# Adding every expert block's result to one line per token in DRAM, and the last LayerNorm's statistics on ACT

## What is computed

```python
def moe_ffn(h, ...):                 # t: 1024 tokens x 1024
    scores = sigmoid(t @ w_router)   # 64 experts
    _, idx = top_k(scores + router_bias, 8)
    gate_w = 2.5 * sel / sel.sum(-1)
    ...                              # pairs (token, expert), sorted by expert, in blocks of 128
    yb = (silu(g) * u) @ w_expert_down[e]          # g, u from xblk @ w_expert_gu[e], 256 each
    routed = segment_sum(yb * row_w, row_tok)      # 8 lines are added per token
    shared = (silu(sg) * su) @ w_shared_down
    return routed + shared
y = moe_ffn(modulate(layer_norm(x1), shift, scale), ...)
out = layer_norm(ALPHA * x1 + gate * y) * ln2_g + ln2_b
```

## Time and profile before

| | us |
|---|---|
| median of three runs | 1880.53 |
| the profiled execution | 1878.81 |
| its span | 1877.0 |
| TensorE busy | 1775.9 (95%) |
| VectorE busy | 1126.2 (60%) |
| ACT busy | 763.3 (41%) |
| GpSimd busy | 726.1 (39%) |
| GpSimd's DMA queue (q0) | 73.57 MB, 15.3% of 16 engines' span |
| SP's queue (q1) | 298.45 MB, 41.8% |

### The profile page before, as it was taken

The page is one execution under the profiler, slowest core; times in us unless marked ns, Lnnn a source line. Parts: engine busy times, 40 slices in busy tenths (PEclk is TensorE's granted clock), DMA queues, the critical chain, the costliest instruction groups (busy, mean ns, idle before and its releaser), DMA issues.

```text
span 1877.0 us, 33114 instructions
## 1 busy us (share of the span) xinstructions
PE 1775.9 (95%) x7478; PEld 1247.1 (66%) x7479; DVE 1126.2 (60%) x1653; ACT 763.3 (41%) x1043; POOL 726.1 (39%) x753
## 2 busy tenths in 40 slices
PE   6999999998889999899999999999999999999966
PEld 1546454446754465478887888888888878888823
DVE  4751766403868644657628898563965784555428
ACT  0210111222230021356638788563865774655400
POOL 2000000004822224635545565554654554555513
PEclk9999999999999999999999999999999999999978
DMA  9752000011343323668648899673987897678794
GB/s 381 268 207 91 1 0 0 0 36 40 113 164 147 144 112 88 195 237 331 241 157 323 313 361 370 236 262 99 359 271 236 278 356 214 189 223 253 221 321 190
DMA packets 113533, 376.76 MB, mean 201 GB/s; under 512 B 34858, under 2 KB 35018, under 8 KB 102739
## 3 DMA queue, kind: packets, MB, share of 16 engines
q1 hardware_dynamic: 65696, 298.45, 41.8%
q0 software_dynamic: 46640, 73.57, 15.3%
q10 hardware_dynamic: 1156, 4.21, 0.6%
HBM read 349.31 MB, written 130.40 MB: 256 GB/s over the span
## 4 chain that ended last, share of the span: by engine, by line
PE 78%; DMA 6%; DVE 5%; issue 3%; ACT 2%; POOL 2%; SPq 1%; DVEq 1%; ACTq 1%; POOLq 0%
PE psum L1286 9%; PE psum L1288 8%; PE psum L1287 8%; PE psum L1029 7%; PE psum L1134 5%; PE psum L1273 4%; PE psum L1307 4%; PE psum L1305 4%; PE psum L1306 4%; PE psum L1038 4%; DMA raw_weights<-in_w_gu 4%; PE psum L1347 3%; PE psum L987 3%; PE psum L1069 3%; PE psum L1188 2%
## 5 line engine op out<-in xcount | busy, mean ns | idle before, releaser
L1796 DVE TENSOR_TENSOR split_weights<-raw_weights,split_weights (+1 forms) x366 | 428.1, 1220 | 34.0 <-ACT split_weights L692 32.2
L692 ACT ACTIVATE split_weights<-raw_weights (+1 forms) x366 | 364.2, 1062 | 21.0 <-SPq L491 12.1
L1286 PE MATMUL psum<-split_weights,split_rows 128*128 (+1 forms) x832 | 334.9, 402 | 0.6 <-DVE split_rows L1785 0.6
L1288 PE MATMUL psum<-split_weights,split_rows 128*128 (+1 forms) x832 | 325.5, 391 | 0.0
L1287 PE MATMUL psum<-split_weights,split_rows 128*128 (+1 forms) x832 | 324.1, 390 | 0.0
L692 ACT ACTIVATE arena<-psum 128x1024 f32<-128x1024 f32 (+4 forms) x200 | 161.3, 811 | 397.6 <-PE psum L1029 107.1
L655 POOL DMA_INDIRECT pair_rows<-arena,idxs x104 | 200.2, 1925 | 35.1 <-issue 31.7
L692 ACT ACTIVATE split_rows<-psum 128x256 fp32r<-128x256 f32 (+1 forms) x209 | 148.4, 710 | 153.4 <-PE psum L1294 150.7
L1288 PEld LDWEIGHTS psum<-split_weights,split_rows 128*128 128x128 f32 x832 | 156.2, 188 | 34.6
L1286 PEld LDWEIGHTS psum<-split_weights,split_rows 128*128 128x128 f32 x832 | 156.9, 189 | 29.6 <-DVE split_rows L1785 0.8
L1287 PEld LDWEIGHTS psum<-split_weights,split_rows 128*128 128x128 f32 x832 | 156.8, 188 | 29.8
(11 more groups left out here) (261 smaller groups left out, 2453.7 us busy)
## 6 DMA issues: line engine op xcount, KB each, us to landing
raw_weights<-in_w_gu SPq DMA_DIRECT2D x62, 2048.0 KB, 11.0
raw_weights<-in_w_dn SPq DMA_DIRECT2D x62, 1024.0 KB, 9.3
arena<-in_w_ada SPq DMA_DIRECT2D x12, 2048.0 KB, 8.8
arena<-pair_rows SPq DMA_DIRECT2D x16, 1024.0 KB, 11.1
arena<-in_toks SPq DMA_DIRECT2D x18, 512.0 KB, 9.8
arena<-job_rows SPq DMA_DIRECT2D x16, 512.0 KB, 3.7
arena<-in_w_vog SPq DMA_DIRECT2D x1, 4160.0 KB, 12.7
arena<-in_w_qk SPq DMA_DIRECT2D x1, 4096.0 KB, 17.8
```

The costliest lines, as they stand in the source:

```text
L692: return act.activation(o, i, ACT.Copy)
L1286: mm(bank(3 + p), xk, part(par, 0, 512 * k), start=(k == 0), stop=False)
L1288: ins = mm(bank(3 + p), xl, part(par, 0, 512 * k), start=False, stop=(k == 7))
L1796: tt(cols(wsplit, (1 - par) * (2 * WE) + (WE + 1024 * c), 1024), cols(raw, (1 - par) * WE + 1024 * c, 1024), high, ALU.subtract).then_inc( ...
```

## The change

- **One line per token.** `y_dram` has 1,024 rows. SP stores the shared expert's tile into it (line 481), and every block adds its rows to it with an accumulating indirect DMA; nothing is stored by blocks. An add waits until the add of the block before has landed. One index column serves gather and add.
- **Order on GpSimd.** Per block: gather of block b+5 first, then the add of block b. Before the loop it waits for the shared lines' stores.
- **No scaling of the shared weights, no `add_shared`.** The lines of `x1_dram` are loaded as they are.
- **The end.** SP loads one line per token (8 transfers of 512 KB). TensorE has nothing to do. VectorE multiplies by the gate row and adds the residual in place; ACT makes the sum of a tile with one pass (`accum_out`), the negative mean, and the sum of squared differences with a second pass; GpSimd makes the reciprocal root; VectorE normalises as before. SP issues the output in ACT's place.

```diff
-                sp.dma_start(shared_dram[P * j:P * j + P, :], yB[:, j % 2, :]).then_inc(S(f"acc_out{j % 2}"), 16)
+                sp.dma_start(y_dram[P * j:P * j + P, :], yB[:, j % 2, :]).then_inc(S(f"acc_out{j % 2}"), 16)
...
             for j in range(NTX):
-                load_pairs(j)
+                sp.dma_start(yres[j], y_dram[P * j:P * j + P, :]).then_inc(S(f"y_in{j}"), 16)
+            for j in range(NTX):
+                sp.wait_ge(S("out_ready"), j + 1)
+                sp.dma_start(out[P * j:P * j + P, :], yres[j]).then_inc(S("out_done"), 16)
...
-            pool.tensor_scalar(g2S, g2S, 1.0 / ALPHA, None, ALU.mult).then_inc(S("prepared"), 1)
-            pool.tensor_tensor(wsd, wsd, g2S.unsqueeze(1).to_broadcast([P, 2, D]), ALU.mult).then_inc(S("prepared"), 1)
-            for j in range(3):
-                add_shared(j)
...
             for q in range(64):
-                if q in (24, 40, 62):
-                    add_shared(3 + (24, 40, 62).index(q))
...
-            def scatter(b, p, nth):
+            def add_rows(b, p, nth, before):
 
                 pool.wait_ge(S("m_y"), b + 2)
-                pool.tensor_copy(idxs[:, 2 * p:2 * p + 2].unsqueeze(2), idxS[:, :].rearrange("p (v n) -> p v n", v=2)[:, :, bass.ds(b, 1)]).then_inc(S("idx_copied"), 1)
+                pool.tensor_copy(idxs[:, p:p + 1], idxT[:, bass.ds(b, 1)]).then_inc(S("idx_copied"), 1)
                 pool.wait_ge(S("idx_copied"), nth)
+                pool.wait_ge(S(f"added{1 - p}"), before)
                 pool.sem_inc(S("passed"), 1)
-                pool.indirect_dma_start(out=y_dram[0:NSUM, :], out_offset=..., in_=yB[:, p], ...).then_inc(S(f"stored{p}"), 16)
-
-            def add_rows(p, before):
-
-                pool.wait_ge(S(f"stored{1 - p}"), before)
-                pool.indirect_dma_start(out=y_dram[0:NSUM, :], ..., compute_op=ALU.add).then_inc(S(f"added{p}"), 16)
+                pool.indirect_dma_start(out=y_dram[:, :], ..., compute_op=ALU.add).then_inc(S(f"added{p}"), 16)
...
+            for i in range(2):
+                pool.wait_ge(S(f"acc_out{i}"), 64)
             with pool.Fori(0, rest) as i:
                 for p in range(2):
 
-                    scatter(2 * i + p, p, 4 * i + (2 * p + 6))
                     pool.wait_ge(S("m_xb"), 2 * i + (p + 4))
-                    gather(bass.ds(2 * i + (p + 5), 1), 1 - p, 4 * i + (2 * p + 7))
-                    add_rows(p, 16 * i + (16 + 16 * p))
-            add_shared(6)
-            add_shared(7)
+                    gather(bass.ds(2 * i + (p + 5), 1), 1 - p, 4 * i + (2 * p + 6))
+                    add_rows(2 * i + p, p, 4 * i + (2 * p + 7), 16 * i + (16 + 16 * p))
...
             for j in range(NTX):
-                act.wait_ge(S("out_ready"), j + 1)
-                act.dma_start(out[P * j:P * j + P, :], yres[j]).then_inc(S("out_done"), 16)
+                act.wait_ge(S("y_ready"), j + 1)
+                act.activation(squares[j % 2], yres[j], ACT.Copy, accum_out=ysum[:, j:j + 1]).then_inc(S("y_step"), 1)
+                act.wait_ge(S("y_step"), 2 * j + 1)
+                act.activation(ymean[:, j:j + 1], ysum[:, j:j + 1], ACT.Copy, scale=-1.0 / D).then_inc(S("y_step"), 1)
+                act.wait_ge(S("y_step"), 2 * j + 2)
+                act.activation(squares[j % 2], yres[j], ACT.Square, bias=ymean[:, j:j + 1], accum_out=yvar[:, j:j + 1]).then_inc(S("y_mv"), 1)
...
-            def combine(j):
-                        ins = mm(o, ident, ybuf[HALF * (j % 4) + k][:, 512 * h:512 * h + 512], start=(k == 0), stop=(k == HALF - 1))
...
             for j in range(NTX):
                 y = yres[j]
-                dve.wait_ge(S("ysum_pe"), j + 1)
-                tt(y, psum[:, 0:1024] if j % 2 == 0 else psum[:, 1536:2560], g2B, ALU.mult).then_inc(S("ysum_read"), 1)
-                link(stt(y, x1_in[j], ALPHA, y, ALU.mult, ALU.add))
-                moments(y, mv[:, 2 * j:2 * j + 2], "y_mv", hst[:, 8:20] if j % 2 else stats)
+                dve.wait_ge(S(f"y_in{j}"), 16)
+                link(tt(y, y, g2B, ALU.mult))
+                stt(y, x1_in[j], ALPHA, y, ALU.mult, ALU.add).then_inc(S("y_ready"), 1)
                 if j >= 1:
                     finish(j - 1)
```

More of the change, by code:

```diff
@@ L86, in constant_tiles @@
     c[:, C_HALF:C_HALF + 16] = -0.5
-    pair = TOPK * (p[:, None, None] + P * np.arange(8)[None, :, None]) + np.arange(TOPK)[None, None, :]
-    c[:, C_TOK:C_TOK + 64] = np.where(pair < NPAIR // 2, pair - NPAIR // 2, pair - NPAIR // 2 + 1).reshape(P, 64)
+    c[:, C_TOK:C_TOK + 64] = np.repeat(p[:, None] + P * np.arange(8)[None, :] + 1, TOPK, axis=1)
     c[:, C_P] = p
@@ L149, in build @@
         idxg = sb("idxg", 2, U32)
-        idxs = sb("idxs", 4, U32)
+        idxs = sb("idxs", 2, U32)
+        ysum, ymean, yvar = (sb(n_, NTX) for n_ in ("ysum", "ymean", "yvar"))
         zrow = sb("zrow", P, parts=RP)
@@ L285, in build @@
         g2B, lg2, lb2 = (at(D0 - WE + i * 1024, 1024) for i in range(3))
-        ybuf = [at(A0 + 1024 * i, 1024) for i in range(4 * HALF)]
+        squares = [at(A0 + 1024 * i, 1024) for i in range(2)]
         yres = [at(A0 + 24576 + 1024 * i, 1024) for i in range(8)]
@@ L665, in _ @@
             rest = pool.value_load(pairs_rest[0:1, 0:1], min_val=NE // 2 - 1, max_val=MAXB // 2 - 1)
+            for i in range(2):
+                pool.wait_ge(S(f"acc_out{i}"), 64)
             with pool.Fori(0, rest) as i:
                 for p in range(2):
-                    scatter(2 * i + p, p, 4 * i + (2 * p + 6))
                     pool.wait_ge(S("m_xb"), 2 * i + (p + 4))
-                    gather(bass.ds(2 * i + (p + 5), 1), 1 - p, 4 * i + (2 * p + 7))
-                    add_rows(p, 16 * i + (16 + 16 * p))
-            add_shared(6)
-            add_shared(7)
+                    gather(bass.ds(2 * i + (p + 5), 1), 1 - p, 4 * i + (2 * p + 6))
+                    add_rows(2 * i + p, p, 4 * i + (2 * p + 7), 16 * i + (16 + 16 * p))
             for p in range(2):
-                scatter(2 * rest + p, p, 4 * rest + (6 + p))
-                add_rows(p, 16 * rest + (16 + 16 * p))
+                add_rows(2 * rest + p, p, 4 * rest + (6 + p), 16 * rest + (16 + 16 * p))
             for p in range(2):
-                pool.wait_ge(S(f"stored{p}"), 16 * rest + 32)
                 pool.wait_ge(S(f"added{p}"), 16 * rest + 32)
@@ L685, in _ @@
             for j in range(NTX):
-                rstd_of((S("y_mv"), NTX + j + 1), mv[:, 2 * j + 1:2 * j + 2], j, "y_rstd")
+                pool.wait_ge(S("y_mv"), NTX + j + 1)
+                pool.tensor_scalar(veps[:, j:j + 1], yvar[:, j:j + 1], 1.0 / D, EPS, ALU.mult, ALU.add).then_inc(S("pool_step"), 1)
+                n["p"] += 1
+                pool.wait_ge(S("pool_step"), n["p"])
+                pool.tensor_tensor(rstd[:, j:j + 1], veps[:, j:j + 1], cst[:, C_HALF:C_HALF + 1], ALU.pow).then_inc(S("y_rstd"), 1)
         @block.scalar
@@ L881, in y_evac @@
                 act.wait_ge(S("block_done"), b + 2)
-                act.wait_ge(S(f"stored{p}"), 8 * (b - p) + 16)
                 act.wait_ge(S(f"added{p}"), 8 * (b - p) + 16)
```

78 lines of the change are left out of this document (14 added, 64 removed).

## The result

The change takes 1860.27 us (median of six runs, 1856.63 to 1868.54), the kernel before on the same chip 1880.53 (six runs, 1877.69 to 1883.03): ratio 0.990, 95% interval 0.9881 to 0.9918. Forecast were 1866 us and a range of 1851 to 1889. The profiled execution took 1861.55 us with a span of 1859.7.

What follows compares the result with a forecast made beforehand. The prediction took TensorE to bound the expert loop, with a separate TensorE-led end. From 1878.8 us, the tail's -24.7, -1.9 ahead of the loop and the loop's +12 gave 1864.2, plus 1.7: 1866 us, range 1851 to 1889.

Steps and rivals of the forecast that it cites:

- Ahead of the loop: Routing before the expert loop: three adds of shared lines no longer delay GpSimd's comparisons by 0.64 us each, -1.9 us.
- The last adds: End of the loop: the last two blocks' adds land at 1791.9 and 1798.0, against 1799.6 before, saving 1.6 us.
- The first tile: Start of the tail: the first line tile loads in 4.3 us, so VectorE starts at 1802.5.
- VectorE's last stretch: Tail: eight tiles on VectorE with stalls for statistics take 45.1 us, ending at 1847.6; the whole tail saves 24.7 us.
- The loop: Expert loop: added rows take more DMA time, costing +12 us, bounds 0 and 25, in blocks that load weights.
- price per row: Expert loop: a row added instead of stored costs 15 ns of DMA time, 61 us over 4,096 rows, mostly hidden.
- The threshold of 8.7 us: Expert loop: no add waits for the one before while adds land within 8.7 us.
- rival B: Dense blocks of the loop: the chain of adds sets the pace, +64 us, 1918 in all; chance 0.13.
- signs of being wrong: Adds waiting over half a microsecond in early dense blocks, loop longer by over 27 us, or end tiles over 6 us.
- The issue beside VectorE's splitting: GpSimd in the loop: a DMA issue beside weight splitting takes 2.50 us, not 1.60, so 0.9 us later.
- The sum: Whole kernel: 1878.8 - 24.7 - 1.9 + 12 = 1864.2 us profiled, plus 1.7 to the median, 1866 us.
- the upper bound of the prediction: Tail: ACT's sum beside its pass costs between 0 and another 0.2 us per instruction.

Runs made afterwards that it cites:

- x4: The kernel before, with each add also waiting for the add of the block before: 1880.03 us, ratio 1.0005 to the kernel before.
- x2: The change, with the add of a block issued ahead of the gather on GpSimd: 1857.58 us, ratio 0.9899 to the kernel before.
- x8: The change, with adds ahead of gathers and VectorE finishing each tile two tiles later instead of one: 1855.88 us, ratio 0.9874 to the kernel before.
- x3: The change, with plain indirect stores in place of accumulating ones, so the sum over experts is left out: 1843.41 us (one run).
- x1: The change, with odd blocks adding to a second set of lines and no waits between adds: 1873.80 us, ratio 0.9959 to the kernel before.
- x5: The change, with a plain read of as many rows and a plain store in place of each add, sum left out: 1884.50 us, ratio 1.0021.
- x7: The change, with mean and variance made by VectorE as before: 1871.50 us, ratio 0.9957 to the kernel before.

## Why the prediction was right, step by step

- **Ahead of the loop**, -1.9 forecast, -1.8 measured. The agreement is luck: block 0 starts 3.8 us earlier than before (795.4 for 799.2), and then takes 12.6 us for 10.6. Most of these 2.0 us are the clock: it is half of full for 3.4 us inside block 0 (0.86 in the mean of the block, 1.00 before), and TensorE is busy 11.24 us there for 9.65. Over all kernels block 0 takes 10.5 and 10.6 us where the clock holds, 11.3 to 13.3 with one such stretch of 3.4 us and 13.4 with one of 6.8. Why its start gained 3.8 and not 1.9 isn't known; x4, which has the code of before up to there, started 2.0 us later than before, so much of it can be chance.
- **The last adds.** I let the adds follow their blocks, 16.0 us from the last block's start to the last landing; it was 16.8. They followed each other instead. The add of 1773.08 took 9.12 us and the next four went as each one ahead landed, 6.9 to 7.4 us apart. I had worked out this wait for dense runs and not for the place where it lies on the path. x2 and x8 take it away: 13.4 and 13.7 us. (The prediction's 1796 for the first load didn't fit its own sum, which has the last landing at 1798.0.)
- **The first tile.** 3.9 us from landing to VectorE's start, 4.5 forecast.
- **VectorE's last stretch.** 45.1 forecast, 43.1 measured. The idle time before the second pair was there in five of the eight tiles, and GpSimd released it: 3.3 us in all, 4.1 forecast. I took GpSimd's pair at its price beside a busy VectorE for every tile; in the first it takes 0.20 + 0.59, which makes the round trip 3.6 us there, and 5.3 in a later tile, for 5.6. The other 1.2 us are VectorE's own work, 39.8 for 41.0: an instruction that waits for nothing can start before the one ahead has ended (line 1789 at 1814.46, the one ahead ends at 1814.54), so the first pair takes 2.4 to 2.5 us and not 2.52, and the second 2.52 and not 2.6. Together with the exit (4.5, not 4.7) the end is 2.0 us better.
- **The loop**, +12 forecast, +11.1 measured; by the table above kernels with the same loop code differ by up to 2 us, so agreement to 0.9 is partly luck. The mechanism was right in its price per row (15 ns, by x3 14.5), in its cause, the DMA engines' time, and in its place, the dense run. What it had wrong is the spread. The 761 rows of the two runs come out, by the reference's routing, as 523 for blocks 26 to 38 and 238 for blocks 20 to 24 (the second longest run by blocks, 73 to 79, has only some 20). At 15 ns they were to cost 7.8 and 3.6 us; blocks 26 to 38 lost 9.0 more than before (17 ns a row, half clock included), blocks 19 to 25 0.5 less. The other 2.6 us came in runs where I allowed next to nothing, and are of the size by which single executions differ. And one term was missing: the lower clock behind TensorE's holes, up to 3.4 us.
- **The threshold of 8.7 us** for an add's landing. The median in the dense run was 8.8, so by rival B's rule this run sat on the edge, and every add waited, 3.7 us in the mean (40.7 / 11). One of the prediction's own signs of being wrong was adds that wait over half a microsecond each in early dense blocks, and it came: I had allowed 0.4 us in six blocks, and 60 adds waited. The sign was badly chosen, because it asks how long GpSimd waits and not who needs what it brings. But a late add only delays GpSimd, whose gathers run five blocks ahead, and ACT, which needs the buffer two blocks later. The rival's step from "adds wait" to "blocks take as long" skipped that slack. x1, x2 and x4 say the waits cost nothing that shows at this size. I had also named TensorE's release by ACT's copy of the results as a sign for the rival; in this trace ACT's waits for adds do feed the chain, and x2, which has none of them, shows that the loop is as long without. x5 suggests that the rival's step holds once stores come later by another transfer.
- **The issue beside VectorE's splitting.** In the loop its median is 1.607 us and its longest 2.641, so some 0.9 to 1.0 us, as the earlier trace rows had it, was the whole price, and 16 of 104 issues took over 2 us. Nothing like the longer hold-up appeared that the rule of the Trainium skill ("SBUF — State Buffer", section "SBUF: two separate sides") would allow. The Trainium skill ties it there to VectorE's two-port modes and, for an instruction with two SBUF inputs as the splits are, to GpSimd instructions that read SBUF; that the shared ports held these issues is shown by no run here.
- **The sum.** 1864.2 against a profiled 1861.55: 2.0 from the end and 0.9 from the loop, against 0.1 ahead of it. The step to the median went the other way, -1.3 and not +1.7; the change's six runs spread over 12 us, those of the kernel before over 5 here, but over 16 in the 23 runs beside x1 to x4. With the add first they spread over 4, with the moments on VectorE and the gather first over 6. Whether the order has to do with the spread isn't shown.

## What to carry to other kernels

Summing in DRAM by accumulating DMAs is priced by DMA time and not by packets or megabytes of payload. It is free where the engines have room (0.27 to 0.52 busy, no hole) and taken from the other transfers where they are full (q0 3.8 points more, q1 4.5 less); so count the rows that fall into the long full stretches, not all of them. A chain of waits on a queue is no loss by itself (182 us of GpSimd's here, none that shows in the loop): ask when the buffer or the rows are needed, and put the chained transfer first on its queue where the chain ends on the path. A final per-tile stage on one engine gains by whole passes moved to an idle engine, and by a lag that covers the round trip (8.9 us and 2.6 us of VectorE's stretch here). And look at the granted clock before a longer stretch is put down to waits alone.

## What the hardware showed that I had not expected

- ACT reads its accumulator in an instruction of its own, 0.19 us, behind every pass with a sum:

```profile
1814.58 1.06 ACT L904 ACTIVATE arena<-arena 128x1024 f32<-128x1024 f32 x1 [15.14 <-DVE arena L1790]
1815.54 0.19 ACT L904 ACTIVATION_READ_ACCUMULATOR arena<-arena 128x1 f32 x1
1815.76 0.20 ACT L906 ACTIVATE ymean<-ysum 128x1 f32<-128x1 f32 x1
1815.99 1.15 ACT L908 ACTIVATE arena<-arena,ymean 128x1024 f32<-128x1024 f32 x1
1817.05 0.19 ACT L908 ACTIVATION_READ_ACCUMULATOR arena<-arena,ymean 128x1 f32 x1
```

  That is the upper bound of the prediction (0.2 per instruction).
- A short hole in TensorE's work can cost more than itself: behind the holes of 1.9 us that ended at 1067.1 and 1555.4 us the clock was half of full for 3.4 us, which is worth up to 1.7 us more each. It need not: x7 had one of 2.1 us (to 1556.8) and kept the full clock. In x1 and x5 such stretches add up to 17.1 and 23.9 us of the loop.
- GpSimd's two small instructions on one column take 0.79 us together with VectorE idle, and 1.7 to 2.5 beside VectorE's passes over SBUF.
